# Two transformer layers of a fused block: their fp32 projections computed as three fp32r products of rounded parts, weights streamed as 1 MB units, the layer loop written out

## What is computed

```python
for l in range(2):
    h = x @ w_in[l]                                    # 1024 -> 2720: q, k, v of four attentions
    o_a, o_b, o_c, o_d = four_attentions(h)            # low-rank, stick-breaking, sliding window, differential
    gates = sigmoid(x @ w_gate[l] + b_gate[l])         # 1024 -> 4096
    merged = sum(gates[n] * (o_n @ w_br_n[l]) for n in "abcd")
    x = layer_norm(ALPHA * x + merged @ w_out[l])      # 1024 -> 1024
    x = layer_norm(ALPHA * x + grouped_moe(x))         # router, then 32 experts
```

## Time and profile before

| what | value |
|---|---|
| median of 3 runs | 2465.53 us |
| profiled execution, first to last instruction | 2463.8 us |
| TensorE busy | 2283.6 us, 93%, 10168 records |
| VectorE busy | 831.3 us, 34% |
| ScalarE busy | 490.2 us, 20% |
| mean granted TensorE clock | 0.972 of full |
| first layer, `c` to second `c` | 1055.2 to 1756.9 us |
| second layer | 1756.9 us to the end |

### The profile page before, as it was taken

How to read it: one execution, slowest core, us unless ns; L and a number is a source line. 1 busy time by engine, 2 the same in 40 slices (tenths; PEclk the granted TensorE clock), 3 DMA queues, 4 the chain that set the end, 5 groups by cost and what they waited for, 6 DMA issues and landing times.

```text
span 2463.8 us, 25868 instructions
## 1 busy us (share of the span) xinstructions
PE 2283.6 (93%) x10168; PEld 1569.8 (64%) x10168; DVE 831.3 (34%) x1478; ACT 490.2 (20%) x904; POOL 37.1 (2%) x82
## 2 busy tenths in 40 slices
PE   6999999999988899999999799999799998799997
PEld 3677778756866599768887443334478885533333
DVE  3332332544632365522225411122313144411213
ACT  2111222331312144412221111000102220200101
POOL 0000000100000000000000000000000000000000
PEclk8999999999997999999999899999899999899999
DMA  9555431311310345453212178877533121578792
GB/s 373 213 205 205 171 126 57 117 69 69 137 69 1 137 165 195 151 204 137 103 69 86 45 311 343 336 304 310 202 141 132 69 82 51 209 306 337 323 385 94
DMA packets 49273, 433.46 MB, mean 176 GB/s; under 512 B 6656, under 2 KB 7936, under 8 KB 16000
## 3 DMA queue, kind: packets, MB, share of 16 engines
q1 hardware_dynamic: 45296, 423.35, 44.1%
q10 hardware_dynamic: 3856, 8.42, 1.0%
HBM read 430.71 MB, written 1.05 MB: 175 GB/s over the span
## 4 chain that ended last, share of the span: by engine, by line
issue 57%; PE 39%; DVE 2%; ACT 1%; DMA 1%; POOL 1%; DVEq 0%; POOLq 0%; SPq 0%; ACTq 0%
PE bank L2428 15%; PE bank L2421 5%; PE bank L3062 5%; PE bank L3064 2%; PE bank L3115 2%; PE bank L2365 1%; PE bank L3117 1%; PE bank L2572 1%; PE bank L2530 1%; DMA ring<-in_early 1%; PE bank L3130 1%; PE bank L3026 1%; PE bank L2542 1%; PE bank L2552 1%; PE bank L2377 0%
## 5 line engine op out<-in xcount | busy, mean ns | idle before, releaser
L2421 PE MATMUL bank<-HT,ring 128*128 128x256 f32 (+1 forms) x1984 | 466.6, 395 | 8.1 <-issue 5.9
L2421 PEld LDWEIGHTS bank<-HT,ring 128*128 128x128 f32 x1984 | 375.1, 191 | 91.7 <-issue 45.2
L2428 PE MATMUL bank<-HT_HI,W_HI 128*128 128x512 f32 (+1 forms) x704 | 239.3, 340 | 8.3 <-DVE ring_lo L1564 4.1
L2428 PE MATMUL bank<-HT_HI,ring_lo 128*128 128x512 f32 (+1 forms) x704 | 240.1, 341 | 0.0
L2428 PE MATMUL bank<-HT_LO,W_HI 128*128 128x512 f32 (+1 forms) x704 | 238.1, 338 | 0.0
L3062 PE MATMUL bank<-ring,TOKENS 128*128 128x512 f32 x416 | 190.2, 600 | 3.7 <-issue 3.7
L1012 ACT ACTIVATE W_HI<-ring 128x2048 fp32r<-128x2048 f32 x66 | 126.4, 1915 | 294.6 <-PE bank L2428 228.4
L1564 DVE TENSOR_TENSOR ring_lo<-ring,W_HI 128x2048 fp32r<-128x2048 f32 x66 | 151.0, 2288 | 52.9 <-ACT W_HI L1012 52.8
L2324 DVE SCALAR_TENSOR_TENSOR tmp<-th,bank 128x256 f32<-128x256 f32 x50 | 21.1, 421 | 413.7 <-ACT th L1356 413.7
L2428 PEld LDWEIGHTS bank<-HT_HI,W_HI 128*128 128x128 f32 x704 | 133.3, 189 | 36.2 <-issue 17.1
L2428 PEld LDWEIGHTS bank<-HT_HI,ring_lo 128*128 128x128 f32 x704 | 134.6, 191 | 14.6
(11 more groups left out here) (473 smaller groups left out, 2794.8 us busy)
## 6 DMA issues: line engine op xcount, KB each, us to landing
ring<-in_early SPq DMA_DIRECT2D x64, 2048.0 KB, 8.4
ring<-in_l_moe_in SPq DMA_DIRECT2D x38, 2048.0 KB, 12.3
ring<-in_l_dense SPq DMA_DIRECT2D x30, 2048.0 KB, 7.8
ring<-in_l_moe_out SPq DMA_DIRECT2D x12, 2048.0 KB, 11.6
slot<-in_l_moe_in SPq DMA_DIRECT2D x10, 2048.0 KB, 8.5
HT<-in_l_moe_in SPq DMA_DIRECT2D x8, 2048.0 KB, 10.6
slot_xg<-in_l_moe_in SPq DMA_DIRECT2D x8, 2048.0 KB, 10.9
ring<-in_l_moe_out SPq DMA_DIRECT2D x14, 1024.0 KB, 11.3
```

Source lines behind the costliest of these rows:

```text
L2421: last = mm(out, w[:, k0 + k, c0:c0 + P], rhs(k), start=k == 0, stop=k == kn - 1)
L2428: last = mm(out, a, b, start=start and n == 0, stop=stop and n == 2)
```

## The change

1. The dense weights of a layer become 36 units of at most 1 MB (`DENSE`), still one per ring slot. A fp32 unit uses the first half of its slot. For all but the branch units, ACT rounds the unit into the upper half of the same slot of `ring_lo` (`rounds`), and DVE subtracts that from the unit into the lower half (`subtracts`). So 32 units per layer are split.
2. Layer input `HT` is split into `X_HI` (ACT) and `HT_LO` (DVE); `MERGED2` likewise, in four pieces, after the last branch.
3. `features`, `c`, `v`, `dfv` and the output product use `three`. `c`, `v` and the output product are cut in halves of the contraction, both token tiles per half.
4. The hardware loops become Python loops, so that all waits are constants. The last layer's `normed_features` is left out, and its gain and bias follow each token tile at once; in the first layer that step (`residual`) moves into the next layer. The loads of the norms' rows move from the layer's start to step n = 4.
5. Branch products, attention, routing and experts are computed as before.

```diff
-DENSE_WIDTHS = (KD * 416, 4096, KD * 384, 4096, 4096, 4096) + 8 * (4096,) + tuple(n * D for n in BRANCH_TILES) + 2 * (4096,)
+HALF = 2048
+DENSE = [("c", 0, 4 * 416), ("c", 1, 4 * 416), ("sbqk", 0, HALF), ("sbqk", 1, HALF), ("v", 0, 4 * 384), ("v", 1, 4 * 384),
+         ("swq", 0, HALF), ("swq", 1, HALF), ("swk", 0, HALF), ("dfv", 0, HALF), ("dfqk", 0, HALF), ("dfqk", 1, HALF)]
+DENSE += [("gate", i, HALF) for i in range(16)]
+DENSE += [("br", i, n * D) for i, n in enumerate(BRANCH_TILES)]
+DENSE += [("out", i, HALF) for i in range(4)]
...
# SP
-            with sp.Fori(0, LAYERS) as L:
+            for L in range(LAYERS):
...
+                        if i >= 4:
+                            sp.wait_ge(*DENSE_DONE[L, i - 4])
+                        elif L:
+                            sp.wait_ge(*MOE_DONE[L - 1, u % 4])
...
# ACT
+            def rounds(L, *units_of):
+                for n in units_of:
+                    u, width = U_LAYERS + L * N_DENSE + n, DENSE[n][2]
+                    loaded(se, u)
+                    act(ring_lo[:, u % 4, HALF:HALF + width], ring[:, u % 4, 0:width], ACT.Copy).then_inc(unit_rounded, 1)
...
+                rounds(L, 7, 8)
                 for i in range(2):
                     evac(SWQT[:, 2 * i:2 * i + 2, :], J_SWQ[i], cat(J_SWQ[i], 2, T))
+                    rounds(L, 9 + i)
                 evac(DFV, J_DFV[0], cat(J_DFV[0], 2, T))
+                rounds(L, 11, 12)
...
 # in gate(i)
                     last.then_inc(*free(job))
+                    if 1 <= i <= 12:
+                        rounds(L, 15 + i)
...
# DVE
+            def subtracts(L, *units_of):
+                for n in units_of:
+                    u, width = U_LAYERS + L * N_DENSE + n, DENSE[n][2]
+                    ve.wait_ge(unit_rounded, split_number(L, n) + 1)
+                    tt(ring_lo[:, u % 4, 0:width], ring[:, u % 4, 0:width], ring_lo[:, u % 4, HALF:HALF + width],
+                       ALU.subtract).then_inc(unit_split, 1)
...
                 scores(0)
+                subtracts(L, 19)
                 weights(0)
                 for n in range(6):
+                    if n < 4:
+                        subtracts(L, 20 + 2 * n)
                     outputs(n)
                     if n < 5:
                         scores(n + 1)
                         if n == 4:
                             gated(0)
+                        if n < 4:
+                            subtracts(L, 21 + 2 * n)
                         weights(n + 1)
+                subtracts(L, DENSE_AT["out", 0])
                 gated(2)
-                gated(3)
-                ve.drain().then_inc(merged2_ready, 1)
+                subtracts(L, DENSE_AT["out", 1])
+                for i in range(4):
+                    gated(3, [i])
+                    if i:
+                        merged_rest(i - 1)
+                merged_rest(3)
+                subtracts(L, DENSE_AT["out", 2], DENSE_AT["out", 3])
...
+                def normed_features(J):
+                    for i in range(4):
+                        ve.wait_ge(x_hi_ready, 4 + L * 4 + i + 1)
+                        for a in range(2):
+                            k = 2 * i + a
+                            ts(HT[:, k, 0:T], PS[J[i][0]][:, a * T:(a + 1) * T], LN_COLS[:, 2, k:k + 1],
+                               LN_COLS[:, 3, k:k + 1], ALU.mult, ALU.add)
+                        ve.drain()
+                        tt(HT_LO[:, 2 * i:2 * i + 2, 0:T], HT[:, 2 * i:2 * i + 2, 0:T], X_HI[:, 2 * i:2 * i + 2, :],
+                           ALU.subtract).then_inc(*free(J[i]))
+                        ve.drain().then_inc(x_split, 1)
...
+                if L < LAYERS - 1:
+                    for t in range(2):
+                        normalise_tokens(t, 1)
+                    subtracts(L + 1, 0)
+                    normed_features(J_XT3)
+                    subtracts(L + 1, 1)
+                else:
+                    for t in range(2):
+                        normalise_tokens(t, 1)
+                        ve.drain()
+                        residual([t])
...
# PE
-                def features(job, w, c0, tiles=2):
+                def features(job, what, i):
+                    w_hi, w_lo = split_unit(what, i, KD, 256)
                     ps = take(job)
-                    for a in range(tiles):
-                        last = project(job, ps[:, a * T:(a + 1) * T], w, c0 + a * P, xt)
+                    for a in range(2):
+                        cut = slice(a * P, a * P + P)
+                        for k in range(KD):
+                            last = three(ps[:, a * T:(a + 1) * T], X_HI[:, k, :], HT_LO[:, k, 0:T], w_hi[:, k, cut], w_lo[:, k, cut],
+                                         k == 0, k == KD - 1)
...
+                if L == 0:
+                    for t in range(2):
+                        emptied(pe, J_XT[2 * t])
+                        emptied(pe, J_XT[2 * t + 1])
+                outs = [take(J_C[t])[:, 0:416] for t in range(2)]
+                for i in range(2):
+                    tokens_half(outs, "c", i, 416, X_HI, HT_LO, J_C if i else None, x_parts_ready)
```

More of the change, by code:

```diff
@@ L1317, in _ @@
                 half_outputs(5)
+                rounds(L, DENSE_AT["out", 1], DENSE_AT["out", 2])
+                for i in range(4):
+                    se.wait_ge(merged2_ready, L * 4 + i + 1)
+                    act(MERGED2_HI[:, 2 * i:2 * i + 2, :], MERGED2[:, 2 * i:2 * i + 2, :], ACT.Copy).then_inc(merged2_rounded, 1)
+                rounds(L, DENSE_AT["out", 3])
                 def scaled(dst, job, k, n):
@@ L1419, in _ @@
             post_rstd(6, 1, 2, 8)
-            with po.Fori(0, LAYERS) as L:
+            for L in range(LAYERS):
                 po.wait_ge(c_squares_ready, L + 1)
@@ L1988, in _ @@
                 last.then_inc(*free(J_SWK[0]))
+                if L:
+                    residual()
+                subtracts(L, 11, 12, 13)
                 ps = full_at(J_DFQK[1])
@@ L2107, in outputs, with gated @@
                         tt(o, o, r, ALU.mult).then_inc(*free(J_OV[n]))
-                def gated(j):
-                    for i in range(4):
+                def gated(j, some=range(4)):
+                    for i in some:
                         job, turned = J_BR[j][i], J_G2[4 * j + i]
@@ L2717, in _ @@
                 last.then_inc(*full(J_XT[i]))
-            with pe.Fori(0, LAYERS) as L:
+            for L in range(LAYERS):
                 def take(job):
@@ L2767, in _, with tokens_half @@
-                release(U_IN)
+                    for a in range(2):
[3 more added lines that the diff above has]
+                                         k == 0, k == KD - 1)
+                    last.then_inc(*full(job))
+                def tokens_half(outs, what, i, width, x_hi, x_lo, jobs=None, ready=None):
+                    w_hi, w_lo = split_unit(what, i, 4, width)
+                    for t in range(2):
+                        own = slice(t * P, t * P + P)
+                        for k in range(4):
+                            kk = i % 2 * 4 + k
+                            if ready:
+                                ready(kk, t)
+                            last = three(outs[t], x_hi[:, kk, own], x_lo[:, kk, own], w_hi[:, k, :], w_lo[:, k, :],
+                                         kk == 0, kk == KD - 1, tokens_first=True)
+                        if jobs:
+                            last.then_inc(*full(jobs[t]))
+                    if not jobs:
+                        last.then_inc(slot_free[dense_unit(L, what, i) % 4], 1)
```

278 lines of the change are left out of this document (166 added, 112 removed).

## The result

The changed kernel took **2394.44 us** (median of 4 runs, 2387.96 to 2400.33) against 2465.72 of the kernel before in the same session (2465.21 to 2467.15): ratio 0.9708, interval 0.9691 to 0.9726, so 71 us less. The forecast was 2381.0 (2360 to 2406). The profiled execution took 2395.3 us, with a span of 2393.5; against the profiled execution of before it is 70.2 us shorter, where the sum had said 84.5.

What follows compares the result with a forecast made beforehand. The prediction took TensorE (PE), busy 93% of the span, as the bound. Its seven terms summed to -84.5 us from the median 2465.5, giving 2381 us, own range 2368 to 2393, wider range 2360 to 2406.

Steps and rivals of the forecast that it cites:

- Term 1: Layer projections and output product: three rounded records per k-step beat plain fp32, 43.3 us a layer, -86.6 us.
- Term 2: Splitting of weight units: hidden in projections, but PE waits for DVE's subtraction in softmax steps 1 to 3, +11.6 us.
- Term 3: Start of the first layer: `c` waits for the split input and the clock falls, +5.1 us (2.4 without the fall).
- Term 4: Edge of the layers: the loop's 4.4 us jump goes, but splitting the input makes PE late, +2.1 us.
- Term 5: Output product: earlier start on the first split piece, pauses between pieces, tiles ending closer together, -0.4 us, +-4.
- Term 6: PE's gaps at gate, projection and expert jobs vanish with constant waits, 6.5 us a layer, -13 us (0 to -25).
- Term 7: End of the run: last layer's transposes and scaling go, gain and bias follow each tile, -3.3 us.
- (a): Rival: clock falls to half at every PE wait for a unit, +16 us, 2397 us, up to 2407; chance 0.17.
- (c): Rival: in-order splitting on ACT and DVE becomes the bound, slower than before from 1.3 us a unit; chance 0.04.

Runs made afterwards that it cites:

- e4: Changed kernel with one plain fp32 product per k-step instead of three in layer projections and output product, splitting kept: 2464.03 us, ratio 1.0007 to the kernel before.
- e7: Changed kernel without TensorE's wait for all four banks of transposed X before a layer's first product: 2383.81 us, ratio 0.9687 to the kernel before.
- e1: Changed kernel with both gate units of the next softmax step subtracted on VectorE before outputs(n): 2382.93 us, ratio 0.9676 to the kernel before.
- e3: Kernel before with its five hardware loops written out as Python loops, products and units unchanged: 2453.77 us, ratio 0.9959 to the kernel before.
- e5: Changed kernel with the output product's first half in banks 1 and 4 instead of 0 and 1: 2390.21 us, ratio 0.9697 to the kernel before.
- e2: Changed kernel with the output product's second half done token tile by tile: 2385.31 us, ratio 0.9676 to the kernel before.
- e8: Changed kernel again, unedited, measured beside later edits on the same chip: 2395.53 us, ratio 0.9719 to the kernel before.
- e6: Changed kernel with four edits together (earlier subtractions, output product by tile, other banks, first product by pieces): 2360.55 us, ratio 0.9592 to the kernel before.

## Why the prediction was right, and where its sum was off

The time was inside the range and of the right sign; the mechanism was the forecast's. The sum was 14 us too large. Two of its terms carry that.

**Term 1, products (-86.6), mis-sized by 6 us.** The price of a record is the distance between starts in a stretch without a gap and at one clock. Timelines of PE, first in the changed kernel (six jobs, from the second record to what follows), then in e4:

```profile
1096.49 0.29 PE L2563 MATMUL bank<-HT_LO,ring_lo 128*128 128x256 f32 x1
...
1130.31 0.93 PE L2971 MATMUL bank<-ident,arena 128*96 128x128 f32 x7
```
```profile
1148.57 27.79 PE L2899 MATMUL bank<-X_HI,ring_lo 128*128 128x256 f32 x128
1176.20 0.59 PE L2998 MATMUL bank<-HT,later 128*128 128x256 f32 x2
```

The first is 287 records in 33.82 us, 117.8 ns each, and so are the starts in the window of the earlier trace rows. The second is 128 plain records in 27.63 us, 215.9 ns each. A step is then 353 ns in three parts and 432 plain: 78 ns saved where the forecast had 86. Both its prices were divisions of something that is no distance. 13.98 us for 64 records is a duration, with the tail of the last record in it, so 437 was 5 too much; and 427 counts every record that reaches into the window of 50 us, of which 425 start in it, so 351 was 2 too little. With what the start of a job costs, a job is 5.72 us (34.33 for the six) and a plain one 6.99, which makes 24 x 1.27 = 30.5 us a layer instead of 33.0. The output product: 22.27 us against the forecast 22.18, 5.7 less than before. `c` at full clock (e7) 9.17 instead of 9.04, `v` 8.46 instead of 8.35: 2.1 and 2.0. Together 40.3 a layer, -80.6. By experiment e4 it is 77; the difference between the two stays open.

**Term 2, unit waits (+11.6): right.** 2.21, 2.26 and 1.94 us in the three steps against 2.2, 2.0 and 1.6: +12.8. e1 takes them away with one moved instruction.

**Term 3, start (+5.1): right.** `c` starts 2.4 us later and runs its first half at half clock, which e7 prices at 2.5: +4.9.

**Term 4, edge (+2.1): right.** Measured +2.0. e3 shows the jump's worth, 3.8 us where the term had 4.4. The term counted on all four pieces being split before `c` starts, and so it is: PE stands 7.6 us behind the transposes, until 1727.02. What it did not ask is whether that must be so. The code at the product waits for one piece at a time; only a wait for all four banks ahead of it makes PE stand for the last, and e7 takes 5.8 us off the edge by removing that.

**Term 5, output product (-0.4), failed: +7.6.** From its start to the gather the layers save only 2.8 and 3.4 us where the product itself saves 5.7: +2.9 and +2.3. And the start waits 2.90 us where it waited 1.67: +1.2 each. Two steps of the term's argument fell. "PE can begin on the first piece about 1.2 us earlier" looked at the data and not at the bank: bank 0 belongs to branch 3's last job, and DVE comes to that job late because the second output unit's subtraction, which itself waits 0.98 us for ACT's rounding, stands ahead of it (e5). And "Its two token tiles now end closer together, which gives 0.5 back before the layer norm" had the sign wrong. With the tiles closer, DVE still has tile 0's normalising and the subtraction of its rounded part (1.23 us, 1.12 idle before it, waiting for ACT) ahead of tile 1's residual add, and tile 1's transposes wait 4.64 us, not 2.14; e2 takes 1.7 of it away, and 2.92 stay. The timeline of DVE there:

```profile
1354.06 0.81 DVE L2273 TENSOR_SCALAR X<-X,ln_mean,ln_rstd 128x1024 f32<-128x1024 f32 x1 [0.67 <-POOL ln_rstd L1518]
1356.00 1.23 DVE L2290 TENSOR_TENSOR X_PARTS<-X,X_PARTS 128x1024 fp32r<-128x1024 f32 x1 [1.12 <-ACT X_PARTS L1403]
1357.14 0.68 DVE L2302 SCALAR_TENSOR_TENSOR X<-X,bank 128x512 f32<-128x512 f32 x1
```

**Term 6, constant waits (-13): its size holds, its cause only in part.** What the other terms leave of -70.3 is -13.6. The written-out loop alone gives 11.3 - 3.8 (the jump, term 4) = 7.5 us (e3). The other 6 us come with the new units: gaps of 0.26 us before a unit's first product stay in e3 and are mostly gone in e4, whose products are as plain as e3's. By starts such a place costs more than its idle row: in e3 64 records and the start of the next unit take 14.24 us (1146.00 to 1160.24), in e4 64 such records take 13.81, so 0.43 us. Seven fewer of them a layer (11 and 4 in the rows of e3 and e4) are an estimated 6.0 us for two layers, which is the remainder. Which instruction made them was not tried.

**Term 7, end (-3.3): right,** -3.4.

The seven measured: -80.6 + 12.8 + 4.9 + 2.0 + 7.6 - 13.6 - 3.4 = -70.3 (term 6 being the remainder). Of the rivals, (a) did not occur: the clock is 1.00 behind each of the six unit waits. Its time, 2397, came close to the result by other means, which the waits and windows tell apart. (c) would have needed 1.3 us a unit; the units show 12.8 / 64 = 0.2. With term 6 as the remainder, the 14 us of the miss are 6 in term 1 and 8 in term 5, and the other terms together come out as forecast within 0.2.

## What to carry to other kernels

When PE gets faster, look where the engines that serve it in order meet a fixed point: a few moved instructions of DVE, two other banks and one wait less were worth 30 us here by the starts within the profiles and 35 by the medians, nearly half of what the change itself brought. Before costing "it can start when its data is there", list everything that the first instruction waits for, its bank and any wait for a whole group ahead of it included. And take a pitch from starts in a stretch with no gap and one clock, for the old product and the new one alike: a duration or a record count of a window is not one, and neither is a long stretch with half clock in it.

## What the runs showed of the hardware

A 128x256 record of rounded parts, each with its own weight load, has a pitch of 117.8 ns at full clock, in the first block and in the layers; a plain fp32 product takes two records of 215.9 ns. The Trainium skill (TensorE: Matmul & The Clock Gate, Back-to-back issue gap) gives N / 2.4 GHz plus 2.5 ns for the gap of an isolated matmul, without room for its weight load, which for 256 columns would be 109 ns; the traces have 117.8 with one, and the measurement decides. A longer stretch misleads: 1056 records of before from 861.8 to 988.0 us give 119.5 ns, because the first of them ran at half clock (window of before):

```profile
861.00:864.40 3.40, 3.17 (x15) 2.80 (x14) 3.15 (x9) 3.40 (x11) 0.00 (x0) 0.50 0.00 0
```

Waits of 1.9 to 2.3 us in the softmax steps left the clock at 1.00 in the changed kernel, six times, and again in e8. Taking waits away did not keep it there: the softmax steps of layer 1 have a stretch at 0.50 from 1889 us in e2, from 1850.8 in e7, from 1949 in e1 and from 1844 in e6, and those of layer 0 one from 1288 in e6. Against the same steps without one, that is about 1.5 us in e2 and e7 and 3.2 in e1; before, the changed kernel, e3, e4, e5 and e8 have none in these steps. What brings them on stays open.

The first block has a place, before the layers and the same in all these kernels, whose clock is not always the same: windows of 80 us (columns as in the windows above), changed kernel first, then e7:

```profile
720.00:800.00 80.00, 61.78 (x274) 48.92 (x273) 24.13 (x59) 18.63 (x46) 0.00 (x0) 0.73 0.00 1
```
```profile
720.00:800.00 80.00, 63.09 (x310) 50.13 (x311) 26.39 (x62) 18.63 (x46) 0.00 (x0) 0.81 0.00 1
```

The profiles of e1, e6 and e7 have the second form, 0.81, and start the layers' first transposes at 1044.6 to 1046.8 us; the seven others, the kernel before among them, have 0.72 or 0.73 and start them at 1051.2 to 1053.2. So 4 to 9 us of a run are decided there, by nothing that an edit changed. Each of the three executions was also the shortest of its kernel (2375.94, 2359.49, 2380.18). PE is idle nearly a quarter of that stretch, in many short gaps. The kernel before does the same: of its sixteen executions beside e1 to e4, seven took 2457.3 to 2460.1 us with a mean granted clock of 0.974 or 0.975, and nine took 2465.0 to 2467.1 with 0.972 or 0.973. What tips it stays open. For a gain of a few microseconds the starts of steps inside one profile were the better measure.
